# First feed-forward layer: third and fourth weight blocks split between the first token half's root and the layer norm's second half of bias adds

## The reference, cut to what matters

```python
def _layernorm(x, g, b, eps=1e-5):
    mu = jnp.mean(xf, axis=-1, keepdims=True)
    xc = xf - mu
    var = jnp.mean(xc * xc, axis=-1, keepdims=True)
    y = xc * lax.rsqrt(var + eps) * g + b

def rms_norm(x, g):
    y = xf * lax.rsqrt(jnp.mean(xf * xf, axis=-1, keepdims=True) + NORM_EPS)

def swiglu(x, w_in, w_out):          # w_in: 1024 x 5632, w_out: 2816 x 1024
    gate, up = jnp.split(x @ w_in, 2, axis=-1)
    return (jax.nn.silu(gate) * up) @ w_out
```

## Time and profile before

| what | value |
|---|---|
| median of 3 runs | 3501.97 us (3499.13 to 3510.43) |
| profiled execution | 3501.97 us, span in the profile 3500.3 us |
| PE busy | 3250.1 us, 93% of the span |
| DVE, ACT, POOL busy | 2051.0, 1275.2, 401.4 us |
| mean granted clock of PE | 0.964 of full speed |

### The profile page before, as it was taken

How to read it: one execution, slowest core, us unless ns; L and a number is a source line. 1 busy time by engine, 2 the same in 40 slices (tenths; PEclk the granted TensorE clock), 3 DMA queues, 4 the chain that set the end, 5 groups by cost and what they waited for, 6 DMA issues and landing times.

```text
span 3500.3 us, 38493 instructions
## 1 busy us (share of the span) xinstructions
PE 3250.1 (93%) x15304; PEld 2556.8 (73%) x15304; DVE 2051.0 (59%) x2723; ACT 1275.2 (36%) x1880; POOL 401.4 (11%) x436
## 2 busy tenths in 40 slices
PE   8988888999899999889999999898878989999998
PEld 7755575778677787567888887685566768888877
DVE  5555546555454545657777664676564677777334
ACT  2554425441433414463332323413424442323123
POOL 1001000120301203020000002340011310000012
PEclk9999999999999999989999999999979999999999
DMA  6210100212402121132223434422064332224233
GB/s 150 48 39 8 49 26 27 59 49 61 67 25 72 43 66 55 37 123 94 85 74 107 137 110 133 129 79 82 1 91 137 114 115 85 85 73 151 98 118 103
DMA packets 344882, 280.31 MB, mean 80 GB/s; under 512 B 52128, under 2 KB 313728, under 8 KB 344416
## 3 DMA queue, kind: packets, MB, share of 16 engines
q1 hardware_dynamic: 322480, 196.30, 19.7%
q0 software_dynamic: 22224, 81.56, 7.2%
HBM read 221.46 MB, written 52.82 MB: 78 GB/s over the span
## 4 chain that ended last, share of the span: by engine, by line
PE 74%; DVE 10%; ACT 7%; issue 5%; DMA 3%; POOL 1%; SPq 1%; ACTq 0%; DVEq 0%; POOLq 0%
PE PS L356 40%; PE PS L2186 13%; PE PA L2186 7%; PE PS L853 2%; PE PB L1602 2%; PE PA L864 1%; DVE WL L325 1%; DMA DEC<-ssd_decay_sums 1%; DVE XL L1865 1%; PE PA L396 1%; PE PB L876 1%; ACT PP L964 1%; DMA WS<-in_ffn_w_out_dram 1%; DVE XST L657 1%; PE PA L1596 1%
## 5 line engine op out<-in xcount | busy, mean ns | idle before, releaser
L356 PE MATMUL PS<-XH,WH 128*128 128x512 f32 x1744 | 612.8, 411 | 53.8 <-DVE WL L325 27.1
L356 PE MATMUL PS<-XL,WH 128*128 128x512 f32 x1744 | 585.4, 395 | 0.0
L356 PE MATMUL PS<-XH,WL 128*128 128x512 f32 x1744 | 583.2, 393 | 0.0
L318 ACT ACTIVATE WH<-WS 128x1024 fp32r<-128x1024 f32 (+1 forms) x235 | 231.9, 990 | 897.2 <-PE PS L356 855.7
L356 PEld LDWEIGHTS PS<-XH,WH 128*128 128x128 f32 x1744 | 331.5, 191 | 155.9 <-DVE WL L325 33.3
L356 PEld LDWEIGHTS PS<-XL,WH 128*128 128x128 f32 x1744 | 333.5, 191 | 71.1 <-issue 2.2
L356 PEld LDWEIGHTS PS<-XH,WL 128*128 128x128 f32 x1744 | 332.4, 191 | 71.2
L325 DVE TENSOR_TENSOR WL<-WS,WH 128x1024 fp32r<-128x1024 f32 (+1 forms) x235 | 272.5, 1160 | 190.4 <-ACT WH L318 190.1
L356 PE MATMUL PS<-TQH,WH 128*128 128x512 f32 x448 | 163.0, 399 | 9.0 <-DVE WL L325 8.3
L356 PE MATMUL PS<-TQL,WH 128*128 128x512 f32 x448 | 160.9, 394 | 0.0
L356 PE MATMUL PS<-TQH,WL 128*128 128x512 f32 x448 | 160.7, 394 | 0.0
(11 more groups left out here) (652 smaller groups left out, 6139.9 us busy)
## 6 DMA issues: line engine op xcount, KB each, us to landing
RAW<-in_ffn_w_in_dram SPq DMA_DIRECT2D x36, 1024.0 KB, 5.8
WS<-in_ffn_w_out_dram SPq DMA_DIRECT2D x48, 512.0 KB, 4.1
WS<-in_ssd_w_in_dram SPq DMA_DIRECT2D x40, 512.0 KB, 3.9
DEC<-ssd_decay_sums SPq DMA_DIRECT2D x32, 512.0 KB, 3.7
WS<-in_ffn_w_in_dram SPq DMA_DIRECT2D x32, 512.0 KB, 4.0
TQF<-ffn_hidden POOLq DMA_DIRECT2D x14, 1024.0 KB, 7.6
x_residual<-ACC POOLq DMA_DIRECT2D x6, 2048.0 KB, 7.7
WS<-in_w_mix_in_dram SPq DMA_DIRECT2D x22, 512.0 KB, 3.8
```

The source lines that it names most:

```text
L318: nc.scalar.activation(WH[:, s, 0:cols], WS[:, s, 0:cols], ACT.Copy).then_inc(W_HI[s], 1)
L356: last = nc.tensor.matmul(PS[s][0:width, c], w[:, s, k * width:(k + 1) * width], x[:, k, c], start=(k == 0 and j == 0), stop=(k == kt - 1 ...
```

## The change

ACT splits the weights of block 3 and block 4 between the root of the first token half and the bias adds of the second half, where it did so behind the silu of the first pair. DVE writes the low part of block 4 as soon as it has read the result of block 2, ahead of the first pair's product. All of it is for the first feed-forward layer alone. (`split` is true for the first layer norm, so the new lines run once.)

```diff
@@ ln_scalar @@
         for h in range(2):
             if h == 1 and not split:
                 pre_rstd(act, st, 0, 0)
+                split_hi(act, B_FFN1 + 2)
+                split_hi(act, B_FFN1 + 3)
             for k in range(KT):
@@ ffn_gated @@
         nc.scalar.activation(T[0][:, c], T[0][:, c], ACT.Silu).then_inc(GATE_SILU, 1)
-        if not last:
+        if not last and b != B_FFN1:
             split_hi(act, b + 2)
             split_hi(act, b + 3)
@@ ffn_hidden @@
         v.tensor_tensor(T[1][:, d], PS[u][:, c], RPRE[:, c], ALU.mult).then_inc(PS_READ[u], 1)
+        if b == B_FFN1:
+            split_lo(dve, b + 3)
         dve.wait_ge(PS_READ[u], times(b + 1))
         dve.wait_ge(GATE_SILU, 8 * turn + n + 1)
         v.tensor_tensor(T[1][:, d], T[1][:, d], T[0][:, d], ALU.mult).then_inc(HID_RAW, 1)
-        if not last:
+        if not last and b != B_FFN1:
             split_lo(dve, b + 3)
```

## The result

| kernel | median (range) | ratio to the kernel before, 95% interval | profiled span |
|---|---|---|---|
| before | 3499.13 us (3495.03 to 3510.43, 11 runs) | | 3500.3 |
| changed | 3495.06 us (3489.19 to 3499.89, 11 runs) | 0.9981 (0.9972 to 0.9990) | 3493.4 |
| changed, a second set | 3493.19 us (3488.34 to 3500.12, 12 runs) | 0.9978 (0.9968 to 0.9989) | 3492.4 |

The second set ran beside 19 runs of the kernel before (median 3501.63). The change is worth some 0.2%, 4 to 8 us by the medians of these sets, forecast 7.0. Single executions of one kernel scatter over 10 us, so the trace of the seam is the sharper instrument, and the rest goes by it.

What follows compares the result with a forecast made beforehand. PE was taken as the bound, idle while ACT's bias adds and silu delayed block 3's weights. Terms 6.8 - 1.3 + 1.9 + 2.04 - 1.9 - 0.5 gave 7.0 off 3501.97, so 3495.0 us, range 3490.5 to 3500.5.

Steps and rivals of the forecast that it cites:

- Term 1: Block 3: ACT's high part follows the Exp directly, so PE starts 6.8 us earlier and idle shrinks from 7.64 to 0.8.
- Term 2: ACT ahead of block 4's high part: an added wait of half a microsecond for block 2, second half's high parts 0.7 late.
- Term 3: Block 5: held by DVE's read of block 3, new PE idle of 2.3 to 3.3 us, some 5.5 of 6.8 left.
- Term 4: Blocks 5 to 7: clock falls in block 5, costing 1.9 us; block 7 follows block 6 at once with no fall.
- Term 5: End of first half: sums behind block 7 wait for POOL's seventh sum and start at 1538.2, 7.0 us earlier.
- The sum: Block 3 to the sums behind block 7: 6.8 - 1.3 + 1.9 + 2.04 - 1.9 - 0.5 = 7.0 us gained.
- Lost further down: Rival: idle ahead of block 13 and the DVE chain behind it take the gain back, 3501 to 3502 us; chance 0.07.
- Only moved: Rival: only block 3's idle is moved, clock falls in blocks 5, 7 and at 13, gain 2 to 4 us; chance 0.12.
- More: Rival: PE's clock, low in part of block 3, doesn't fall at shorter stretches, gain 8 to 10.5 us; chance 0.06.
- The clock stays low: Rival: PE stays at 1.2 GHz from block 5 on; four low blocks would give 3514.6 us; chance 0.04.

Runs made afterwards that it cites:

- The last experiment on the edit's parts: Changed kernel with block 4's high part on ACT behind two second-half bias adds; sums behind block 7 37.33 us after those inside block 2, 37.56 in the changed kernel.
- block 3 alone: Against the changed kernel, block 4's high part stays behind the silu and its low part behind the first product; median 3493.58 us, ratio 0.9984 to the kernel before.
- The filler: Changed kernel plus eight unread matmuls behind block 4; sums behind block 7 37.59 us after those inside block 2, 37.56 in the changed kernel.
- short sums: Changed kernel with POOL adding only 8 of 512 columns of second-half squares; sums behind block 7 37.22 us after those inside block 2, 37.56 in the changed kernel.

## Why the prediction was right, step by step

- **Term 1** (block 3 6.8 us earlier, idle 0.8). Measured 12.79 - 5.95 = 6.84, idle 0.81.
- **Term 2** (ACT waits half a microsecond; silu later, 0.7 for the second half's high parts). The wait was 0.60. Counted from block 2's sums the first such high part moved from 12.33 (1511.97 - 1499.64) to 13.05 (1512.39 - 1499.34): 0.7. The last experiment on the edit's parts showed that this 0.7 goes through to the sums behind block 7, as X contained it. The cover that the term claimed for the loads was there: with block 4 late ACT waits 3.0 for the load of block 6, and with the early copy it doesn't wait for it.
- **Term 3** (DVE reads block 3 at X = 1515.3 or 1516.3; 3.6 us from there to block 5). X was 1514.94, with this trace 0.30 ahead of the old one at the anchor: 1515.24, the lower end, with both low parts at 0.75. That is the value the Trainium skill's rule on shared ports gave ("SBUF — State Buffer", "Who interferes with whom"); the sum had taken the middle. The second low part started at 1514.27, POOL's sum at 1514.84, so the trace agrees. (In the second trace of block 3 alone a low part that started 0.04 ahead of the sum was slowed all the same, so with starts that close the recorded order didn't decide.) To block 5 it was 3.61. PE's new idle stretch was 2.08, forecast 2.3 to 3.3: blocks 3 and 4 had ended when forecast, and X was early.
- **Term 4** (low part of block 6 2.31; read of block 5 at X + 12.5; fall of the clock in block 5 and none in block 7; block 7 at X + 16.4). Measured 2.31, X + 12.78, ten matmuls at 0.54 in block 5, none in block 7, and block 7 at once behind block 6, which ended its last matmul at 1531.30, X + 16.4. The four low parts took 5.84, forecast 5.4, so block 7's low part was ready at 1531.27, X + 16.3 for the X + 16.1 forecast: DVE and PE came level there. The fall itself came as forecast in both traces of the changed kernel, but the other traces don't bear out a rule by the length of the stretch alone (last section).
- **Term 5** (the sums behind block 7 at X + 22.4, held 0.5 by POOL's last sum). This one was mis-sized: they started at X + 21.96, right behind the matmuls. POOL's last two sums took 3.07, not the 3.78 of the earlier trace rows:

```profile
1533.67 3.07 POOL L1875 TENSOR_TENSOR T<-T,SQQ 128x512 f32<-128x512 f32 x2 [7.07 <-ACT SQQ L1862]
```

- **The sum.** 7.98 at the seam for the 7.0 forecast: 0.55 from X and 0.45 from the sums. Along PE the gain is 6.84 at block 3, 6.06 at block 5 (5.5 forecast), 6.36 at block 7 and 7.98 at the sums behind it. The 6.06 holds a term that the sum has no name for: in the kernel before seven matmuls of block 3 were slow, 1.5 us, which aren't there now. They stand in the recorded 12.66 of blocks 3 and 4, so the -1.3 at block 5 is 1.5 won and 2.8 of new idle. By time the gain is 3499.13 - 3495.06 = 4.1 between the medians, and 6.6 by the ratio of the first set (0.0019 x 3499), 7.7 by that of the second. That the forecast of 3495.0 meets 3495.06 to a tenth is luck: it was counted from 3501.97, 2.8 above the median of all 11 runs before, and the medians are 2.9 less apart than the gain forecast.
- **The rivals.** *Lost further down*: no, 57.22 for 57.26 to the quads, though in the trace of ACT's moves alone 1.6 went there. *Only moved*: no for the changed kernel, but ACT's moves alone come near it, 2.96 gained at the sums. *More*: no; it also counted as extra the low clock in block 3, which the sum held already. *The clock stays low*: no; nine or ten slow matmuls in block 5 took the place of eight or nine in block 7.
- One reading was too simple: the sum books the fall in block 5 as a price of 1.9. The filler took the fall away and nothing was gained, as DVE beside POOL held block 7 at the same time.

## What to carry to other kernels

Where an in-order engine prepares operands for the bottleneck, list what stands ahead of each preparation and move behind it all that is wanted only later; then do the same on the next engine of the hand-over, since much of what an early first half (here ACT's copy) gives can be lost if the second half (DVE's) still stands behind an unrelated wait. Price the result by following the chain to the next late step, not by the idle stretch removed: 6.8 us at block 3 were 6.1 at block 5 and 8.0 behind block 7. Where single executions scatter over more than the gain, measure between two fixed instructions of the trace on either side of the edit, and in two traces, as one can be lucky.

## What the runs showed of the hardware

- The length of an idle stretch on PE didn't settle whether slow matmuls (1.2 GHz) followed. Stretches of 2.04 to 2.08 us were followed by eight to ten in six cases (before, both traces of the changed kernel, short sums, the second trace of DVE's move alone, ACT's moves alone) and by none in three (the first trace of DVE's move alone, both of block 3 alone). The 1.74 to 1.75 ahead of block 13 was followed by none in twelve traces and by eight or nine in one, of ACT's moves alone. Ahead of block 5 the changed kernel's stretch of 2.05 to 2.08 brought them in all three traces that have it, and 0.24 to 1.33 in its place brought none in three.
- DVE's four low parts of the input took 2.73 with almost nothing on POOL beside them, 5.84 to 5.86 or 6.88 to 6.98 with POOL's sums, by how the two meet: the same kernel showed both. With starts 0.04 us apart, DVE ahead, one trace had DVE's first instruction at 0.75 and POOL's at 1.87, the other at 1.88 and 1.30.
- POOL's sums are slowed in turn: two took 3.07 in one meeting with DVE and 3.78 in another; the shortest single one before took 1.28.
